# A two-layer hybrid mixer kernel on one core: the last maximum taken by matmuls, the opening begun with the first tile, the early loads spaced out, and each ring slot loaded in halves

## What is computed

```python
u = rms_norm(x, norm_g)
proj = u @ w_in                              # 1024 -> about 5500 features, in 43 tiles of 128
# group a: causal convolution, then an SSD scan      -> ya
# group b: causal convolution, then an mLSTM scan    -> yb
# group c: latent attention: keys = rms_norm(latents @ w_uk), softmax, context @ w_uv -> yc
# group d: attention over a memory of 256 positions  -> yd
y = concatenate([ya, yb, yc, yd]) @ w_out    # 2048 -> 1024, in 8 tiles of 128
x = x + y
# after both layers: rms_norm(x, final_norm_g)
```

```python
s = (einsum('bqhd,bkhd->bhqk', qn, k_nope) + einsum('bqhr,bkr->bhqk', qr, k_rope)) * scale
p = softmax(s)
ctx = einsum('bhqk,bkc->bqhc', p, lat)
```

## Time and profile before

| | us |
|---|---|
| median of 3 runs (1357.4 to 1366.79) | 1358.81 |
| the profiled execution's own time | 1357.34 |
| its span in the trace | 1355.5 |
| PE busy in the span | 1274.3 (94%) |
| DVE / ACT / POOL busy | 604.1 / 426.9 / 212.6 |

### The profile page before, as it was taken

The page is one execution under the profiler, slowest core; times in us unless marked ns, Lnnn a source line. Parts: engine busy times, 40 slices in busy tenths (PEclk is TensorE's granted clock), DMA queues, the critical chain, the costliest instruction groups (busy, mean ns, idle before and its releaser), DMA issues.

```text
span 1355.5 us, 22216 instructions
## 1 busy us (share of the span) xinstructions
PE 1274.3 (94%) x6868; PEld 1055.7 (78%) x6868; DVE 604.1 (45%) x1335; ACT 426.9 (31%) x1029; POOL 212.6 (16%) x388
## 2 busy tenths in 40 slices
PE   5999999799999999979989999997999999999797
PEld 4877777588888888867877867776787888888585
DVE  3253125445555555553213611344475555555512
ACT  0131225225444444430013212422443444444300
POOL 0000022001132223300000001400002333330000
PEclk9999899999999999999999999999999999999898
DMA  7445342217155555502474443302453444444032
GB/s 281 149 133 172 111 155 65 88 63 243 65 167 168 169 168 170 171 32 70 147 274 150 161 160 114 119 27 82 154 190 110 164 156 162 157 161 145 16 125 94
DMA packets 82680, 186.76 MB, mean 138 GB/s; under 512 B 15708, under 2 KB 51333, under 8 KB 70935
## 3 DMA queue, kind: packets, MB, share of 16 engines
q1 hardware_dynamic: 60710, 104.48, 23.1%
q0 software_dynamic: 17280, 72.90, 16.0%
q10 hardware_dynamic: 4608, 8.39, 1.6%
HBM read 171.79 MB, written 13.93 MB: 137 GB/s over the span
## 4 chain that ended last, share of the span: by engine, by line
PE 74%; issue 11%; DMA 6%; SPq 3%; DVE 2%; ACT 1%; POOLq 1%; POOL 1%; DVEq 0%; ACTq 0%
PE ps L623 21%; PE ps L528 20%; PE ps L960 9%; PE ps L610 3%; DMA ring<-in_weights 3%; SPq L300 2%; PE ps L717 2%; PE ps L725 2%; DMA states<-in_mlC 2%; PE ps L641 2%; PE ps L763 1%; PE ps L557 1%; PE ps L549 1%; PE ps L839 1%; PE ps L601 1%
## 5 line engine op out<-in xcount | busy, mean ns | idle before, releaser
L623 PE MATMUL ps<-wk,scr 128*128 128x258 f32 x2048 | 470.8, 383 | 0.0
L623 PEld LDWEIGHTS ps<-wk,scr 128*128 128x128 f32 x2048 | 381.3, 191 | 53.8 <-issue 3.3
L528 PE MATMUL ps<-uT,ring 128*128 128x264 f32 (+1 forms) x1344 | 310.5, 395 | 7.7 <-DMA ring<-in_weights 7.7
L528 PEld LDWEIGHTS ps<-uT,ring 128*128 128x128 f32 (+1 forms) x1344 | 250.0, 192 | 60.9 <-DMA ring<-in_weights 9.7
L1288 DVE TENSOR_REDUCE ssq<-scr 128x4 f32<-128x512 f32 x256 | 170.7, 682 | 160.4 <-ACT scr L1032 159.9
L1032 ACT ACTIVATE scr<-ps 128x512 f32<-128x512 f32 x256 | 151.7, 593 | 2.5 <-DVE ssq L1288 2.5
L465 POOL DMA_DIRECT2D kr<-in_krope x256 | 135.3, 530 | 88.1 <-issue 75.7
L1029 ACT ACTIVATE raws<-ps 128x4 f32<-128x4 f32 x256 | 44.6, 174 | 290.5 <-PE ps L623 290.5
L439 POOL DMA_DIRECT2D ring<-in_weights x64 | 34.9, 545 | 614.0 <-PE ps L528 419.4
L960 PE MATMUL ps<-pt,ring 128*128 128x264 f32 x512 | 118.5, 394 | 4.5 <-DVEq L1733 4.5
L960 PEld LDWEIGHTS ps<-pt,ring 128*128 128x128 f32 x512 | 98.7, 194 | 21.8 <-DVEq L1733 4.8
(11 more groups left out here) (313 smaller groups left out, 1252.2 us busy)
## 6 DMA issues: line engine op xcount, KB each, us to landing
ring<-in_weights POOLq DMA_DIRECT2D x60, 1024.0 KB, 5.3
lat<-in_lat SPq DMA_DIRECT2D x256, 128.0 KB, 3.2
rows<-rowscr SPq DMA_DIRECT2D x16, 1024.0 KB, 7.7
lat<-in_weights SPq DMA_DIRECT2D x8, 1024.0 KB, 6.6
kr<-in_krope POOLq DMA_DIRECT2D x256, 32.0 KB, 2.2
uT<-in_memv SPq DMA_DIRECT2D x16, 512.0 KB, 5.8
uT<-in_memk SPq DMA_DIRECT2D x16, 512.0 KB, 5.8
states<-in_ssm SPq DMA_DIRECT2D x16, 256.0 KB, 3.9
```

The source lines that it names most:

```text
L528: last = mm(ps[part, bank, 0:T], w[:, k, 0:ROPE] if m == KR else w[:, k, :], u3[:, k, :], start=k == 0, stop=k == KT - 1)
L623: last = mm(ps[:, 1 + 2 * (j % 2) + half, 0:258], latT[:, g % 2, q, c, :], wk[:, 2 * c + half, at:at + 258], start=c == 0, stop=c == 1)
```

## The change

It has five parts.

1. **Ring slots in halves.** Each slot has two semaphores. `half_chunk` loads one half (512 KB, one input tile or half an output tile), as soon as the tile that used that half is done. In the output stage a new signal `o_half` frees the first half in the middle of a tile. POOL's and PE's loops over chunks and output tiles are written out.
2. **Loads spaced.** SP waits for the end of input tile 0 before the memory tokens, of tile 4 before `wk`, of tile 7 and tile 13 before the two memory chunks, and of tile 17 before `wsm`.
3. **The opening (layer 0).** SP loads the norm's weight, then the two halves of x, then the constants. DVE makes `xg` first, while ACT squares x; DVE adds the squares in two steps and PE adds the last two parts and the partitions in the middle of tile 1. PE starts tile 0 with the first part of `xg`.
4. **The last maximum.** For sample 7 POOL is left out. PE turns the 128x8 maxima by a matmul with the identity, DVE reduces and puts the 8 values on a diagonal, PE spreads them with a matmul of ones, and DVE copies them back.
5. **Order at the layer's end.** ACT takes the root for the last keys before the two group squares, and saves the last states after the exponentials. DVE copies the context before it scales group b. PE runs `by_feature` before it waits for `mixed`, and output tile 0's first half is no longer split.

```diff
+            def half_chunk(l, at, n, a, free, wide=1024):
+                pool.wait_ge(*free)
+                weights = d["weights"][CHUNKS * l + n]
+                pool.dma_start(ring[:, at % 2, a * 1024:a * 1024 + wide], weights[:, a * 1024:a * 1024 + wide]
+                               ).then_inc(slot_in[at % 2][a].sem, 16)
+
+            def in_chunk(l, at):
+                n = RING_IN[at]
+                for a in range(1 if at in NO_SECOND else 2):
+                    if at < 2:
+                        free = (o_mm if a else o_half)(l, at - 1)
+                    elif at - 2 in (AT_QK, AT_V):
+                        free = tok_mm(l, 3 if at - 2 == AT_QK else 7)
+                    else:
+                        tile = min(2 * RING_IN[at - 2] + a, IN_TILES - 1)
+                        free = pj_mm(l, TILE_ORDER.index(tile) + 1)
+                    half_chunk(l, at, n, a, free, 512 if at == AT_V else 1024)
...
+                sp.wait_ge(*pj_mm(l, 1))
                 sp.dma_start(memn, d["memT"]).then_inc(mem_in.sem, 16)
...
-                sp.dma_start(wsm[:, :, :].rearrange("p a n -> p (a n)"), small[:, 1024:3072]).then_inc(wsm_in.sem, 16)
+                sp.wait_ge(*pj_mm(l, 5))
                 sp.dma_start(wk[:, :, 2:258], small[:, 0:1024].rearrange("p (a n) -> p a n", a=4)).then_inc(wsm_in.sem, 16)
+                sp.wait_ge(*pj_mm(l, 8))
                 load_big(l, R_MK, 0)
-                load_big(l, R_MK, 1)
-
...
+                sp.wait_ge(*pj_mm(l, 14))
+                load_big(l, R_MK, 1)
+                sp.wait_ge(*pj_mm(l, 18))
+                sp.dma_start(wsm[:, :, :].rearrange("p a n -> p (a n)"), small[:, 1024:3072]).then_inc(wsm_in.sem, 16)
...
-                        if a == 0 and k == 0:
-                            pe.wait_ge(*xg_ready(l, KT - 1))
-                        if a == 0 and k == KT // 2:
+                        if a == 0 and (l == 0 or k == 0):
+                            pe.wait_ge(*xg_ready(l, max(k + 1, KT - 1 if l else 0)))
+                        if l and a == 0 and k == KT // 2:
                             x_sum(l - 1, KT - 1).then_inc(x_ss.sem, 1)
...
+                        if l == 0 and a and k == KT // 2:
+                            pe.wait_ge(first.sem, 16)
+                            pe.wait_ge(*x_sq(-1, KT))
+                            mm(ps[:, 4, 0:T], ones, u3[:, 0, :], start=True, stop=False)
+                            mm(ps[:, 4, 0:T], ones, u3[:, 1, :], start=False, stop=True).then_inc(x_ss.sem, 1)
...
+                pe.wait_ge(*mx_in(l, NB))
+                mm(ps[0:8, 6, P:2 * P], sm[:, 1, 0:8], ident, start=True, stop=True).then_inc(mx_t.sem, 1)
                 sums(l, 8, 0, [[(P, nsq_ssd[:, 2 * i + j, :]) for j in range(2)] for i in range(2)])
+                pe.wait_ge(*mx_d(l, 1))
+                mm(ps[:, 6, 256:264], ones[0:8, :], sm[0:8, 0, 48:56], start=True, stop=True).then_inc(mx_b.sem, 1)
                 sums(l, 9, 2, heads(1))
...
+                by_feature(l)
                 pe.wait_ge(*mixed(l, 1))
-                out_tile(0, 0, 0, MIX_EARLY // 2)
-                by_feature(l)
-                out_tile(0, 0, MIX_EARLY // 2, MIX_EARLY)
+                out_tile(0, 0, 0, MIX_EARLY)
...
+            def last_max(l):
+
+                dve.wait_ge(*mx_t(l, 1))
+                red(sm[0:8, 0, 40:41], ps[0:8, 6, P:2 * P], AXX, ALU.max)
+                dve.drain()
+                ts(sm[0:8, 0, 48:56], ident[0:8, 0:8], sm[0:8, 0, 40:41], None, ALU.mult).then_inc(mx_d.sem, 1)
+                dve.wait_ge(*mx_b(l, 1))
+                copy(sm[:, 1, 8:16], ps[:, 6, 256:264])
+                dve.drain()
...
+                dve.wait_ge(*cx_mm(l, NB))
+                copy(ctxr, ps[:, 7, 128:512]).then_inc(cx_out.sem, 1)
                 dve.wait_ge(*n_rs(l, 10))
```

111 lines of the change are left out of this document (57 added, 54 removed).

## The result

| | before | after |
|---|---|---|
| profiled execution | 1357.34 us (span 1355.5) | 1344.74 us (span 1343.0) |
| median of the runs shown with the result | 1362.8 (4 runs) | 1342.6 (4 runs, 1340.6 to 1344.7) |
| ratio | 1 | 0.9874 [0.9837, 0.9912] |
| mean granted clock of the profiled execution | 0.975 | 0.972 |

The change makes the kernel 17 us faster by the ratio (1.3%), and 12.5 us between the two profiled executions. The forecast was 24.1 us and 1334.7; the time lies just outside the range.

A forecast was written before the change was run, and what follows sets the result against it. PE was taken as the bound, busy 94% with about 81 us idle. Opening 7.7, ring 9.4 and layer ends 7.0 sum to 24.1 us off 1357.3, 1333.2, plus 1.5 for the median: 1334.7, 8-in-10 range 1325 to 1342.

The forecast's parts named there:

- Opening: Start of layer 0: x's second half lands earlier and tile 2 starts sooner, winning 7.7 us, bounds 3 and 9.
- Ring: Ring loads: all five PE waits go, 7.7 us, and 1.75 of clock, winning 9.4 us, lower bound 0.
- POOL issues twice as many ring loads: POOL's ring loads: about 0.5 us each, all beside its waits for tiles, so no cost was charged.
- the three terms: The gains forecast for the opening, 7.7 us, the ring, 9.4, and the layer ends, 7.0, together 24.1 us.
- Layer ends: End of both layers: matmul maximum and new order win 8.4 us, less 1.4 for clock: 7.0, bounds 0 and 12.
- the 1.4 that was charged: Layer ends: charge for both layers in case PE's longer wait ahead of the sums lowers the clock.
- 1.84: Output tile 0: us per layer it would gain if the clock stayed up; none of it counted.
- A: Rival: the ring's waits stay or move, costing the same 9.4 us in other places; 1344 us, chance 0.09.
- B: Rival: the layer ends give nothing, the clock staying low, with a loss of 1.1 us per layer; 1344, chance 0.08.
- C: Rival: at the layer ends the matmul route is as slow as POOL, only `by_feature` (1.2) won; 1340.5 us, chance 0.04.
- D: Rival: ring half loads each late, slower than before; at 12.2 us per half 77 us slower, 1436; chance 0.02.

The follow-up runs named there:

- whole_loads: The changed kernel with each ring slot loaded whole (1024 KB) as before, SP's loads still spread out: 1354.8 us, ratio 0.9960.
- unspaced: The changed kernel with SP's loads of the input stage in one burst again, ring halves kept: 1340.2 us, ratio 0.9857.
- warm_behind_decay: The changed kernel with one extra unread POOL reduction per layer, between POOL's first and second scaling of states: 1329.8 us, ratio 0.9775.
- filled_half: The changed kernel with warm_pool's extra reduction and 6 and 4 calls of unread matmuls in PE's two layer-end waits: 1333.1 us, ratio 0.9785.
- pool_max: The changed kernel with the last maximum back on POOL's reduction over partitions, the rest of the layer's end as changed: 1349.9 us, ratio 0.9915.
- warm_pool: The changed kernel with one extra unread POOL reduction over partitions per layer, ahead of POOL's first scaling of states: 1336.9 us, ratio 0.9837.

## Why the prediction was nearly right and still missed

**Opening, 7.7 forecast, 7.0 in the trace (5.7 when undone).** Within its bounds, but not by the steps as written. x's second half landed at 8.48, earlier than the 10.4 I took. But the prediction had tile 0's first half computed under that transfer, and never asked when its weights come: the first ring load landed only at 7.95, so PE started there and all 24 first records followed it, 7.93 us, where 24 at the full rate take 5.4. The two errors cancelled, so that the 7.0 is close to the 7.7 by luck.

```profile
7.95 7.93 PE L585 MATMUL ps<-xc,ring 128*128 128x264 f32 x24 [7.95 <-DMA ring<-in_weights]
...
19.49 10.70 PE L559 MATMUL ps<-uT,ring 128*128 128x264 f32 x47 [0.94 <-DVE uT L1477]
```

**Ring, 9.4 forecast, 8.9 in the trace.** Right: waits from 7.7 to 0.8. The term lay in the halves, as `whole_loads` shows. The spread loads, which the text named as part of it, contributed nothing (`unspaced`).

**The step that failed: "POOL issues twice as many ring loads, about 0.5 us each, all beside its waits for tiles".** That was priced at nothing, because the only cost I looked for was POOL's own time. The loads also lengthen the gap ahead of POOL's next reduction, by 0.085 us each: with 23 more loads in layer 0 (81 against 58) and 29 in layer 1 the gap grew by 1.9 and 2.2 us, and the path of the first sample's maximum has no slack there, so PE stood 1.8 and 2.1 us longer. Behind the longer waits its records ran slower too, by 1.5 and 1.0 us. So this step cost 6.4 us in the trace. `whole_loads`, which takes the loads back, and `warm_behind_decay`, which covers the gap, both show PE's wait shrink again, and in both the 32 records of layer 0's context take 1.93 us in place of 3.00. A sign of it was in the trace of before, as the same gap of 10.87 ahead of the first reduction and 7.3 to 7.9 ahead of the later ones. I had read POOL's reductions only at the layer's end.

**The clock.** Of the 5.3 us of longer busy time ahead of sample 1, 2.5 belong to the step above. The rest lies in stretches where the same records ran at a granted clock of 0.94 and 0.95 in place of 0.97. The forecast started from the profiled 1357.3, which was also the fastest run shown of before, and added 1.5. Executions of the same PE work differ by up to 5 us of busy time, so this part of the miss belongs to no step of the prediction. By the ratio, which is not tied to these two executions, 17 us were won, 7 less than forecast: 6.4 for POOL's answer and 2.0 for the three terms (22.1 for 24.1) are 8.4, and the difference of 1.4 is well inside the interval of 5 us to either side.

**Layer ends, 7.0 forecast, 6.2 in the trace.** Layer 1 gave 4.6 for 4.3 and layer 0 gave 1.5 for 4.05. The maximum is read 3.0 us after its reduction in layer 1, as foretold (3.1), and 4.64 in layer 0, where the sums ran at the low clock: 1.5 us longer, close to the 1.4 that was charged. Output tile 0 took 6.24 and 5.51 us for its 16 records (at 0.225 each, 3.6), at a granted clock of 0.50 to 0.54 in layer 0, the lower of PE's two levels (1.2 GHz). The prediction had left 1.84 of this in, by counting no gain there (5.4 us for the 16), so only 0.8 us in layer 0 was not priced. The wait of 2.2 us ahead of the tile had stayed, and `filled_half` shows that filling PE's waits ends the slow rate. `pool_max` (7.2 us slower) bears the term out.

**The rivals.** A fell: the ring's waits did not move. B happened by a part in layer 0 only. C fell: the matmul route took 3.0 and 4.6 us; the rule of the Trainium skill ("GPSIMD Engine Reference", section "Engine selection") that gives such reductions to GpSimd stands against `pool_max`, in which they cost 7.2 us more. D fell: the one half load that PE waited for in layer 0's input stage took 11.7 us, and cost 0.8 us. The rule of "DMA: Bandwidth & Descriptors" (section "Measured (HBM→SBUF, 128 partitions, SWDGE, issued from GpSimd)") in the Trainium skill, to batch loads, does not hold for this kernel's time: halving them won 12.2 us. What each further load did cost here was another thing: time on the engine that issues it, at its next reduction.

## What to carry to other kernels

Ask of every instruction added to a queue what stands behind it in that queue, hundreds of instructions later too: here the price of 23 more loads was paid by the first reduction after them. When a warm-up or any other cover is placed in an engine's idle time, read in the trace which instruction ends that time, or the wait only moves. And where PE, which bounds this kernel, had to wait for 2 to 3 us, work that nobody reads in that wait made the records behind it faster, if it ended before the wait did; that was worth 0.0052 of the ratio over `warm_pool` once, and twice as much of it nothing.

## What was unexpected of the hardware

- The gap between POOL's copy and its reduction over partitions grows with the loads that POOL issued since the last such reduction, from 5.9 us (none) to 14.6 us (105), and is 10.1 with 130 and 10.2 with 154.
- An extra reduction ahead occupied POOL for 26 us, from 306.18 to 332.13, not only for the 13.7 ahead of its own record.
- Behind a wait of 2.2 us a tile of 16 records took 5.5 and 6.2 us in the changed kernel; with PE's waits at the layer's end filled it took 3.8.
- The first 512 KB load issued by POOL at 1.45 landed at 7.9 to 8.0 with three more issued right behind it and without them, while x's first half (528 KB), issued by SP at 1.31, landed at 5.1. Issued by ACT at 0.85, the same load took 4.0 us.
